# Second normalisation moved into the expert loop of a hybrid decoder trunk, with partial sums scattered and gathered

## What is computed

```python
x = LayerNorm(alpha * x + concat(A, B) @ w_o)          # first normalisation
x = LayerNorm(alpha * x + HMoE(x))                     # second normalisation
# HMoE: top-1 of 4 groups, then top-2 of the 8 experts in that group
h = jax.nn.silu(xb @ w_gate[e]) * (xb @ w_up[e])       # 1024 -> 512, 32 experts
y[token] += gate * (h @ w_down[e])                     # 512 -> 1024, two experts per token
```

## Time and profile before

| | us |
|---|---|
| median of 3 runs | 2217.98 |
| lowest and highest | 2217.72, 2220.22 |
| the profiled execution | 2221.0 |
| its span in the profile | 2219.2 |
| PE busy | 2058.5 (93%) |
| DVE busy | 704.0 (32%) |
| ACT busy | 382.3 (17%) |
| POOL busy | 298.3 (13%) |

### The profile page before, as it was taken

How to read it: one execution, slowest core, us unless ns; L and a number is a source line. 1 busy time by engine, 2 the same in 40 slices (tenths; PEclk the granted TensorE clock), 3 DMA queues, 4 the chain that set the end, 5 groups by cost and what they waited for, 6 DMA issues and landing times.

```text
span 2219.2 us, 31577 instructions
## 1 busy us (share of the span) xinstructions
PE 2058.5 (93%) x12532; PEld 1233.7 (56%) x12532; DVE 704.0 (32%) x1370; ACT 382.3 (17%) x984; POOL 298.3 (13%) x312
## 2 busy tenths in 40 slices
PE   8999999989999999989599999999999989998990
PEld 5666655566555655545366666555765546544550
DVE  4412166671111111111482123767411111111116
ACT  2001123301211111111110111332011111211110
POOL 1200011111111111111331000110011111110104
PEclk9999999999999999989799999999899999998995
DMA  6610013358999999999434110223689999999964
GB/s 226 182 39 29 19 42 116 133 199 317 366 379 383 402 366 382 375 378 345 170 115 115 38 39 11 90 79 130 262 340 367 381 390 380 376 377 372 380 260 158
DMA packets 75368, 527.44 MB, mean 238 GB/s; under 512 B 14554, under 2 KB 23642, under 8 KB 50290
## 3 DMA queue, kind: packets, MB, share of 16 engines
q1 hardware_dynamic: 62162, 491.52, 57.5%
q0 software_dynamic: 13056, 33.84, 6.2%
HBM read 486.21 MB, written 54.60 MB: 244 GB/s over the span
## 4 chain that ended last, share of the span: by engine, by line
PE 88%; DVE 5%; issue 4%; ACT 1%; DMA 1%; POOL 0%; DVEq 0%; SPq 0%; POOLq 0%
PE ps L570 19%; PE ps L869 18%; PE ps L912 10%; PE ps L710 9%; PE ps L865 5%; PE ps L857 5%; PE ps L551 4%; PE ps L840 3%; PE ps L906 2%; PE ps L919 2%; PE ps L891 2%; PE ps L754 1%; PE ps L800 1%; PE ps L657 1%; PE ps L681 1%
## 5 line engine op out<-in xcount | busy, mean ns | idle before, releaser
L570 PE MATMUL ps<-arena 128*128 128x344 f32 x1440 | 421.1, 453 | 0.0
L871 PE MATMUL ps<-arena 128*64 128x256 f32 x1792 | 418.1, 389 | 0.0
L869 PE MATMUL ps<-arena 128*64 128x256 f32 x1792 | 418.0, 389 | 0.0
L570 PEld LDWEIGHTS ps<-arena 128*128 128x128 f32 x1440 | 272.0, 190 | 142.9 <-issue 3.6
L869 PEld LDWEIGHTS ps<-arena 128*64 128x64 f32 x1792 | 237.0, 135 | 164.7 <-issue 23.6
L912 PE MATMUL ps<-arena 128*64 128x512 f32 x448 | 241.4, 689 | 54.7 <-issue 54.6
L914 PE MATMUL ps<-arena 128*64 128x512 f32 x448 | 241.8, 690 | 0.0
L871 PEld LDWEIGHTS ps<-arena 128*64 128x64 f32 x1792 | 236.4, 134 | 0.0
L1830 POOL DMA_INDIRECT ytok<-arena,gidx x64 | 94.0, 1468 | 986.6 <-ACT arena L1165 374.2
L1606 DVE SCALAR_TENSOR_TENSOR arena<-ps,gates,arena 64x256 f32<-64x256 f32 (+1 forms) x128 | 61.1, 477 | 475.2 <-ACT arena L1142 475.2
L710 PE MATMUL ps<-arena 128*128 128x512 f32 x448 | 195.9, 594 | 4.8 <-ACT arena L1090 4.8
(11 more groups left out here) (243 smaller groups left out, 2079.9 us busy)
## 6 DMA issues: line engine op xcount, KB each, us to landing
arena<-in_w_gate SPq DMA_DIRECT2D x64, 2048.0 KB
arena<-in_w_up SPq DMA_DIRECT2D x64, 2048.0 KB
arena<-in_w_down SPq DMA_DIRECT2D x64, 2048.0 KB
arena<-in_w_in SPq DMA_DIRECT2D x36, 512.0 KB, 3.5
arena<-out_y_all SPq DMA_DIRECT2D x16, 512.0 KB, 3.5
xs<-arena SPq DMA_DIRECT2D x16, 512.0 KB, 2.7
ytok<-arena SPq DMA_DIRECT2D x16, 512.0 KB, 3.6
arena<-ytok SPq DMA_DIRECT2D x16, 512.0 KB, 7.5
```

The lines of the kernel that those rows point to most:

```text
L570: last = mm(ps[:, 3 * half + ch, 0:CH], wring[:, slot, k * P:(k + 1) * P], xT[:, k, ch * CH:(ch + 1) * CH], start=(k == 0), stop=(k == KD ...
L869: mm(ps[HALF:P, 2 + q, 0:256], xgT[:, slot, k, 0:HALF], wg_half[slot3][q][:, k], start=(k == 0), stop=(k == KD - 1))
L871: last = mm(ps[0:HALF, 2 + q, 0:256], xgT[:, slot, k, 0:HALF], wu_half[slot3][q][:, k], start=(k == 0), stop=(k == KD - 1))
```

## The change

The second normalisation is done for each expert's rows inside the loop, for those tokens whose second (later) expert this is.

- A token's two experts come at two turns of the loop. At the first, the result is added on DVE to the token's row, which the gather has brought (`summed`), and the sum goes to `ytok` by a plain scatter (`part_scatter`). At the second, `part_gather` reads that partial sum over the row in the input buffer, DVE adds the result, and the row is complete.
- `part_gather(e)` waits until `part_scatter(e−1)` has landed, and `summed(e)` on DVE waits for `part_gather(e)`. Statistics follow in `summed`; `shifted(e)` (subtraction of the mean) stands between the two halves of the gating of expert e+1; POOL computes the inverse root (`inverse`); `normalised2(e)` does the last pass; and `final_scatter(e)` writes the rows to `y_all`.
- Which rows are first and second visits is computed once per layer by more DVE instructions and 18 matmuls (`visits`, on PE between expert 0's gate and up and the transposition of its hidden values). The gathers for experts 2 and 3 wait for these matmuls.
- The input buffers are four instead of two, two of them in the place of the first normalisation's parameters. `gather(e+3)` is issued behind `final_scatter(e−1)`.
- POOL issues four indirect DMAs per expert: part gather, final scatter, gather, part scatter. No DMA adds any more.
- The stage behind the loop is gone. SP waits for the final scatters, and for layer 1 it loads the tiles of `y_all`; the projection weights are issued ahead of these loads. PE's first transpositions wait for the loads and no longer for DVE. The old normalisation is kept inside the overflow branch.

```diff
+NXG = 4
+def rows_of(n):
+    return P if n // 2 in (0, EARLY_PAIRS + 1) else (MID, HALF)[n % 2]
+
+
+def place(n):
+    pair = n // 2
+    if pair in (0, EARLY_PAIRS + 1):
+        return n % 2 + (FIRST if pair else 0)
+    return (FULL, WIDE)[n % 2] + pair - (1 if pair <= EARLY_PAIRS else 2)
...
+        xgs = [lnp[:, 0], lnp[:, 1], xg[:, 0], xg[:, 1]]
+        xg_by_row = [x.rearrange("t (p k) -> t k p", k=KD) for x in xgs]
...
+                    sp.wait_ge(s[f"ln_out{n}"], 16 * (NE // 2) * (l + 1))
                     settle(sp, s["sp_passed"])
-                    sp.dma_start(a["y_all"][l + 1, t * P:t * P + tile_rows(t), :], xin[t][0:tile_rows(t)]
-                                 ).then_inc(s["x2_out"], 16)
-
-                sp.wait_ge(s["x2_out"], BASE + 16 * NT * (l + 1))
-                settle(sp, s["sp_passed"])
+                if l < DEPTH - 1:
+                    for t in range(NT):
+                        sp.dma_start(xin[t][0:tile_rows(t)], a["y_all"][l + 1, t * P:t * P + tile_rows(t), :]
+                                     ).then_inc(s[f"l2_in{t}"], 16)
...
-                    pe.wait_ge(s["x2_ready"], BASE + NT * l + t + 1)
+                    pe.wait_ge(s[f"l2_in{t}"], BASE + 16 * (l + 1))
...
+                pe.wait_ge(s["rk_turn"], BASE + l + 1)
+                mm(ps[:, 3, 128:128 + NE], ones[0:NE], dturn, start=True, stop=True).then_inc(s["rk_turns"], 1)
...
+                def visits():
+                    pe.wait_ge(s["rk_visit"], BASE + l + 1)
+                    for k in range(2):
+                        for t in range(NT):
+                            last = mm(ps[:, 5, 256:256 + 2 * NE], slot_of(k, t),
+                                      block_visit[:, k, t].rearrange("p q n -> p (q n)"),
+                                      start=(k == 0 and t == 0), stop=(k == 1 and t == NT - 1))
+                    last.then_inc(s["rk_visited"], 1)
...
                     gate_up(e, 0, slot3[0], turn3[0], first, m)
+                    if e == 0:
+                        visits()
                     hidden_turned(e, 0, first, m)
...
+                def visits():
+                    tt(by_turn, turn_row.unsqueeze(1).unsqueeze(1).broadcast_to([P, 2, NT, NE]), chosen[:], ALU.mult)
+                    op(v.tensor_reduce(turns, by_turn, AX.X, ALU.add))
+                    for k in range(2):
+                        step.mark(v.tensor_tensor(visited[:, 0, k], turns[:, k], turns[:, 1 - k], ALU.is_gt))
+                    step.mark(v.tensor_tensor(by_turn, iota[:, 0:NE].unsqueeze(1).unsqueeze(1).broadcast_to([P, 2, NT, NE]),
+                                              turns.unsqueeze(3).broadcast_to([P, 2, NT, NE]), ALU.is_equal))
...
+                    tt(visited, visited, token[:].unsqueeze(1).broadcast_to([P, 2, 2, NT]), ALU.mult)
+                    for q in range(2):
+                        step.mark(v.tensor_tensor(block_visit[:, :, :, q], by_turn,
+                                                  visited[:, q].unsqueeze(3).broadcast_to([P, 2, NT, NE]), ALU.mult))
+                    step.wait()
+                    dve.sem_inc(s["rk_visit"], 1)
+
+                def visit_rows():
+                    dve.wait_ge(s["rk_visited"], BASE + l + 1)
+                    ts(visit_f, ps[:, 5, 256:256 + 2 * NE], float(NONE), None, ALU.add)
+                    step.mark(v.tensor_copy(visit[:].rearrange("p q n -> p (q n)"), visit_f))
+                    ts(final_f, visit_f[:, 0:NE], float((l + 1) * T), None, ALU.add)
+                    op(v.tensor_copy(rki[:, 0:NE], final_f))
+                    dve.sem_inc(s["visit_ready"], 1)
...
                         v.scalar_tensor_tensor(hid[0:live, cols], up, gates[0:live, ds(col, 1)], sg[0:live, cols],
                                                ALU.mult, ALU.mult).then_inc(s["h_ready"], 1)
+                        if q == 0 and e:
+                            shifted(e - 1)
...
+                def summed(e):
+                    n = NE * l + e
+                    r, x = slice(0, rows_of(e)), xgs[e % NXG]
+                    dve.wait_ge(s["y_a"], BASE + n + 1)
+                    dve.wait_ge(s["y_d"], BASE + n + 1)
+                    if e:
+                        dve.wait_ge(s["part_in"], 16 * ((NE - 1) * l + e))
+                    else:
+                        dve.wait_ge(s["xg_mm"], BASE + n + 3)
+                    v.tensor_tensor(x[r], x[r], ys[r, e % 2], ALU.add).then_inc(s["sum_done"], 1)
+                    dve.wait_ge(s["sum_done"], BASE + n + 1)
+                    for h in range(2):
+                        step.mark(v.bn_stats(stat[r, 6 * h:6 * h + 6], x[r, h * 512:(h + 1) * 512]))
+                    step.wait()
+                    dve.wait_ge(s["l2_rstd"], BASE + n - 1)
+                    v.bn_aggr(mv[r, e % 2], stat[r]).then_inc(s["l2_stat"], 1)
+
+                def shifted(e):
+                    n = NE * l + e
+                    r, x = slice(0, rows_of(e)), xgs[e % NXG]
+                    dve.wait_ge(s["l2_stat"], BASE + n + 1)
+                    v.scalar_tensor_tensor(ys[r, e % 2], x[r], mv[r, e % 2, 0:1], lnp[r, 2], ALU.subtract, ALU.mult
+                                           ).then_inc(s["l2_shift"], 1)
+
+                def normalised2(e):
+                    n = NE * l + e
+                    r = slice(0, rows_of(e))
+                    dve.wait_ge(s["l2_shift"], BASE + n + 1)
+                    dve.wait_ge(s["l2_rstd"], BASE + n + 1)
+                    v.scalar_tensor_tensor(ys[r, e % 2], ys[r, e % 2], rstd[r, e % 2, 0:1], lnp[r, 3], ALU.mult, ALU.add
+                                           ).then_inc(s["l2_done"], 1)
 
                 xg_evict(0, 0, P)
...
+                visits()
+                for e in range(NE):
+                    rows = rows_of(e)
+                    hidden(e, rows, (e // 2 - (0 if e < 2 * EARLY_PAIRS + 2 else 1)) if rows == MID else None)
+                    ht_evict(e, rows)
+                    if e < NE - 1:
+                        xg_evict(e + 1, (e + 1) % 2, rows_of(e + 1))
+                    if e:
+                        normalised2(e - 1)
+                    else:
+                        visit_rows()
+                    y_evict(e, e % 2, rows)
+                    summed(e)
+                shifted(NE - 1)
+                normalised2(NE - 1)
...
-                def statistics2(t, r, p):
...
-
-                def normalised2(t, r, p):
...
-
-                rows_at = [slice(0, P if t < NB else NS) for t in range(NT)]
-                statistics2(0, rows_at[0], 0)
-                for p in range(1, NT):
-                    statistics2(p, rows_at[p], p)
-                    normalised2(p - 1, rows_at[p - 1], p - 1)
-                normalised2(NT - 1, rows_at[NT - 1], NT - 1)
...
+                def part_gather(e):
                     n = NE * l + e
...
+                    rows = rows_of(e)
+                    pool.wait_ge(s["xg_mm"], BASE + n + 3)
+                    pool.wait_ge(s["part_out"], 16 * n)
                     settle(pool, s["pool_passed"])
...
+                    g.indirect_dma_start(out=xgs[e % NXG][0:rows], out_offset=None, in_=a["ytok"][0],
+                                         in_offset=bass.IndirectOffsetOnAxis(ap=visit[0:rows, 0, e:e + 1], axis=0),
+                                         bounds_check=T - 1, oob_is_err=False).then_inc(s["part_in"], 16)
+
+                def part_scatter(e):
+                    rows = rows_of(e)
+                    pool.wait_ge(s["sum_done"], BASE + NE * l + e + 1)
+                    settle(pool, s["pool_passed"])
                     g.indirect_dma_start(out=a["ytok"][0],
-                                         out_offset=bass.IndirectOffsetOnAxis(ap=gidx[0:rows, col:col + 1], axis=0),
-                                         in_=ys[0:rows, slot], in_offset=None, compute_op=ALU.add,
-                                         bounds_check=T - 1, oob_is_err=False).then_inc(s[f"sc_out{slot}"], 16)
+                                         out_offset=bass.IndirectOffsetOnAxis(ap=visit[0:rows, 1, e:e + 1], axis=0),
+                                         in_=xgs[e % NXG][0:rows], in_offset=None,
+                                         bounds_check=T - 1, oob_is_err=False).then_inc(s["part_out"], 16)
+
+                def inverse(e):
+                    n = NE * l + e
+                    r = slice(0, rows_of(e))
+                    pool.wait_ge(s["l2_stat"], BASE + n + 1)
+                    settle(pool, s["pool_passed"])
+                    step.link(g.tensor_scalar(rstd[r, e % 2, 1:2], mv[r, e % 2, 1:2], EPS2, None, ALU.add))
+                    g.tensor_tensor(rstd[r, e % 2, 0:1], rstd[r, e % 2, 1:2], mhalf[r], ALU.pow).then_inc(s["l2_rstd"], 1)
+
+                def final_scatter(e):
+                    rows = rows_of(e)
+                    pool.wait_ge(s["l2_done"], BASE + NE * l + e + 1)
+                    settle(pool, s["pool_passed"])
```

(53 more changed lines are left out.)

221 lines of the change are left out of this document (109 added, 112 removed).

## The result

The changed kernel takes **2328.2 us** (median of 4 runs, 2306.1 to 2332.7) against 2217.9 for the kernel before (2214.4 to 2220.2): ratio **1.048**, 95% interval 1.041 to 1.055, slower. Forecast were 2249 and a range of 2165 to 2325. The profiled execution took 2331.9 us with a span of 2330.1; the one before had 2221.0 and 2219.2.

The account below looks back on a forecast made before the run. The loop was taken as one part PE-bound and two parts DMA-bound, with 50.2 us of second normalisation behind it. Sum: 2221.0 − 37 − 5 + 5 + 68 = 2252, less 3.0 for the median: 2249; range 2165 to 2325.

Parts of the forecast that it names:

- signs named under "right": Some 13 us PE-idle end; pairs at 37 or more throughout; DVE's addition waiting for DMA; loop DMA share below 0.94.
- DMA floor: Expert loops: 36.6 us of DMA engine work per pair of experts, against today's mean of 34.6.
- End of the kernel: From the last matmul to the end: 50.2 us become 13, −37 us.
- Between the layers: Last y copy to layer 1's first projection: about 20 to 21 us in place of 26, −5 us.
- Routing: Added matmuls and DVE passes for routing, making PE wait in expert 0: +5 us for both layers.
- DVE in the loop: Expert loops: DVE gains 5.3 us per expert, costing nothing while its inputs come in time.
- DMA volume: Expert loops: plain transfers replace accumulating ones, 4.5 us becoming 4.0; −0.5 us per DMA-bound pair.
- hidden-chain rival: Expert loops: two links together under 16 to 18 us, so the loop keeps its period; 2171 us, chance 0.28.
- The new chain: Expert loops: part scatter and part gather in series, taken at 37.0 us per pair; +34 us per layer, 68 in both.
- upper end: Expert loops: chain priced at the average DMA load, T = 41.7 us per pair.
- chain at its loaded price: Rival, expert loops: 42 us per pair, +104 us a layer, 2389 us; chance 0.18 including results nearer it than the forecast.

Follow-up runs that it names:

- with the chain cut: Changed kernel, part gather reading an array nobody writes in the loop, without waiting for the part scatter's landing: 2212.2 us, ratio 0.998.
- the run with a light DVE: Changed kernel with second-normalisation statistics, subtraction and last pass on DVE cut to 64 columns per instruction: 2328.1 us, ratio 1.050.

## Why the prediction was wrong

The sign was right, and so were steps 1, 2 and 4 and layer 0 of step 3. The signs named under "right" came too: a short end, DVE waiting in the addition for a DMA, a DMA share under 0.94. But the weight lay elsewhere. Of its +34 us a loop the forecast gave 28 to the DMA floor and 6 to the chain; of the +86 measured in the first loop, 17.5 are left with the chain cut, and 68.5 go with it. The chain's term was taken at the wrong one of two values that stood in the text, and the DMA volume's had the wrong sign.

1. *End of the kernel.* Right: 15.0 us behind the last y copy, forecast 13, gain 35 for 37. The rows that the step named are there; in the changed kernel the copy of y, the addition and the last pass are

```profile
2315.06 0.71 DVE arena L1707
...
2315.85 1.23 DVE arena L1718
...
2320.87 1.29 DVE arena L1738
```

  Between the end of the addition (2317.08) and the last pass lie 3.8 us of statistics, aggregate and POOL's inverse root, for which the prediction's figures (1.30, 0.2 and 1.25) give 2.75 and the handoffs.

2. *Between the layers.* Right: 20.7 us where 20 to 21 were forecast. The landing of the final scatter took 3.24 (4.2 was the bound), the loads of x 3.4.

3. *Routing.* The size was right in layer 0, +2.6; layer 1 up to its loop became 4.5 shorter instead of 2.5 longer. Of the 4.5, 2.5 lie in the first 16 matmuls of its projection, 7.39 us before and 4.87 after. Over the first 28.6 us of that layer the granted clock was 0.91 before and 1.00 after. The other 2.0 are open. From the chain that ended last, before and then after:

```profile
1101.42 7.39 PE ps L551 x16
```

```profile
1184.34 4.87 PE ps L586 x16
```

4. *DVE in the loop.* Right: the run with a light DVE gained nothing, and with half the weights all its passes fitted into a loop that PE fills to 99.6%.

5. *DMA volume.* **Wrong in sign.** Priced by the share that POOL's queue takes for itself, the change saved 0.5 us per pair, and the queue's own share did fall, from 12.3 to 11.1% in the run with the cut chain. But the weights' packets take longer beside more rows: 88.6% of 400 us for 136.01 MB are 2.61 us per MB, against 2.51 in the earlier trace rows. A pair loads 12.6 MB, so that is +1.2 us per DMA-bound pair, +0.7 with the −0.5. The step had counted live rows only, 330 a pair; the two programs issue 320 rows a pair before and 640 after, dead ones included, and POOL's queue had 8911 packets in place of 4416. The loops agree in direction and roughly in size: without the chain 595.2 us, or 1.25 more per pair than the 577.7 before, and with 32 rows as well 572.3 (498.19 to the last y copy at 1070.44), at 2.57 us per MB. The hidden-chain rival's 2171 held, to 4 us, only with the added rows gone.

6. *The new chain.* **The step that failed.** The prediction gave T = 22.2 + 22.2 × 36.6/T = 41.7 us per pair as the upper end and the floor as the lower, and then took 37.0, "near the DMA floor", since a waiting PE should leave "quiet gaps just where the chain's transfers run". Measured are (663.7 − 93.8)/14 = 40.7 us per pair in layer 0 and 39.4 in layer 1. 37.0 gave +34 a layer, 40.7 gives +86. The gaps are there, 12% of the DMA engines' time in 600 to 1000 us, just the share that the formula spreads evenly (36.6/41.7 is 88% loaded). And the chain's transfers do run through them, but only because they run through everything: from the first part gather at 541.12 to the last addition at 1164.46 one of them is under way in 560 of 623 us. The mean DMA share beside them is 0.85, that of the whole stretch too. So a link finds the average load, as the formula had it, and the reason for going 4.7 us below its 41.7 was wrong; the two loops came out 1.0 and 2.3 below. Here are five links in a row (part scatter, part gather, part scatter, part gather, part scatter), columns as in the stage rows:

```profile
669.13:678.67 9.54, 8.28 (x28) 3.71 (x28) 4.63 (x8) 0.85 (x2) 2.99 (x3) 0.58 0.60 255
678.67:687.27 8.60, 8.60 (x106) 6.55 (x106) 0.69 (x1) 1.34 (x3) 3.00 (x3) 1.00 0.80 294
...
689.39:693.59 4.20, 3.55 (x25) 2.56 (x23) 3.42 (x8) 1.19 (x4) 1.76 (x3) 1.00 0.66 178
693.59:705.72 12.13, 12.13 (x112) 6.27 (x108) 2.16 (x4) 2.40 (x6) 3.01 (x3) 1.00 1.03 397
...
707.84:719.01 11.17, 9.68 (x74) 4.52 (x78) 5.42 (x9) 1.43 (x3) 2.99 (x3) 0.85 1.01 404
```

  Of all 61 such links of the first loop, the 30 with a share of 0.95 or more take 10.8 us in the median, the 15 under 0.7 take 6.4. A link in a gap is short, but the next one meets the weights again. SP's timeline shows when the loads of weights start (L453 gate, L461 down):

```profile
678.99 0.33 SPq L461 DMA_DIRECT2D arena<-in_w_down  x1
690.62 0.30 SPq L453 DMA_DIRECT2D arena<-in_w_gate  x1
...
699.07 0.34 SPq L461 DMA_DIRECT2D arena<-in_w_down  x1
706.30 0.33 SPq L453 DMA_DIRECT2D arena<-in_w_gate  x1
```

  The part gathers of this stretch start at 678.67 and 693.59, the part scatters at 689.39 and 707.84: three of the four starts of weights have one within 3 us (the one at 699.07 is 5.5 us behind a part gather). By the order of the program PE frees a gate buffer at the end of gate and up, about when the addition and so the part scatter come, and a down buffer at the end of the down projection, about when the next part gather comes. The scatter at 689.39 went out 1.2 us ahead of a bunch and landed after 3.3 us; the one at 707.84, 1.5 us behind, after 10.3. That the bunches are tied to the transfers in this way is read from this timeline, not from a run that moved them.

The rival "chain at its loaded price" (2389, T = 42) had the right period for the chain, but priced a loop at 682 where 663.7 and 645.8 were measured. The measured 2328 lies between it and the forecast, 61 us from the one and 79 from the other, so the case that came is the one given 0.18. The range had no room for the prediction's own upper end either: 41.7 us a pair make 677.6 a loop and 2381 in all, and the range stopped at 2325 ("half way", which would be 2319). The rival "hidden" named a condition, two links under 16 to 18 us together; the run with half of each row fits it, with part scatters that land after 3.6 us and loops that are even.

The Trainium skill's fit for a POOL transfer ("DMA: Bandwidth & Descriptors", section "Anatomy of one DMA — SWDGE (gpsimd) path") gives 2.6 us for 64 rows, an estimate from its formula. That is near the 3.6 of the relieved engines and far from the 8.4 of this kernel; the measurement decides. What the page says under "Queues, rings and completion order", that each DMA engine goes round its queues packet by packet, bears on it: a weight packet takes 77.5% of 16 × 400 us over 8255, 0.60 us, and a part scatter of 64 or 96 rows has 4 or 6 packets and a completion on each engine. That many turns behind a weight packet, on the relieved 3.6 us, would be 6.6 to 7.8, an estimate from these rows against the measured 8.4. But the same count makes 5.4 us of a scatter of 32 rows, and 7.4 and 6.7 were measured in the two runs that had them. So the count of turns is not the whole of it, and how many of the packets that the profile counts go in one turn is not shown.

## What to carry to other kernels

Transfers that were hidden became the bound here once two of them stood in series behind each other's landing in every iteration. Price such a chain at the landing times of the loaded loop, and move off that value only for a gap whose place you can show: a chain that is under way 90% of the time meets the average load. Count the rows that a scatter or gather issues, dead ones too, and look at what they do to the other queue's time per byte, not at their own share alone. To relieve the DMA engines in an experiment, shorten the rows and keep all partitions, and check the queue's share before reading the time.

## What the runs showed that was not expected

- Loads to 64 of 128 partitions run at 214 GB/s of the queue's own time against 388 to 128 partitions, and other queues' transfers land no sooner for it (9.4 against 8.4 us).
- A scatter in which every row is out of bounds and no data move lands after 7.3 us (median) among the weights, where the same scatter with live rows takes 8.4.
- With the weights halved by columns, PE is granted its full clock through the whole loop (1.00, the 2.4 GHz level), against 0.96 before and 0.91 after. After a wait of 9.5 us (until 670.4) PE worked on at a granted clock of 0.50, the 1.2 GHz level, until about 676.6. The down projection began in that time: its matmuls follow each other every 0.85 us there and every 0.43 us afterwards, in PE's timeline:

```profile
674.02 1.06 PE L959 MATMUL ps<-arena 128*64 128x512 f32 x1
...
674.88 1.06 PE L959 MATMUL ps<-arena 128*64 128x512 f32 x1
...
677.72 0.59 PE L959 MATMUL ps<-arena 128*64 128x512 f32 x1
...
678.15 0.59 PE L959 MATMUL ps<-arena 128*64 128x512 f32 x1
```

  The copy of y was done 7.8 us before the addition could start all the same, so this step of the chain didn't get longer by it. PE's 573.5 us busy against 549.8 before are hardly added work: it has 34 matmuls more among 4352.
- POOL's first instruction of the inverse root (L1943) took 1.48 us beside DVE's gating and subtraction at 670.1 and 0.26 at 690.4, two values as far apart as those in the earlier trace rows. In the loop it stayed off the path, since the light DVE gained nothing; at the end of the kernel it took 1.20 us on it.
